# A decay tree's small products, issued in pairs of levels between the main products

## The reference: four blocks of mixer and feed-forward, the last two with two mixers

```python
def gla_chunked(q, k, v, g):      # q, k, g: (B, S, 4, 64); v: (B, S, 4, 128)
    ...
    b = jnp.cumsum(gc, axis=-2)
    diff = b[:, :, :, None, :] - b[:, :, None, :, :]
    decay = jnp.exp(jnp.where(causal[None, None, :, :, None], diff, -jnp.inf))
    attn = jnp.einsum('bhtk,bhsk,bhtsk->bhts', qc, kc, decay)
    o_intra = jnp.einsum('bhts,bhsv->bhtv', attn, vc)
    ...

def hybrid_mixer(h, w_in, ...):
    proj = h @ w_in               # queries, keys, values of both mixers, gates
    ...
    a_out = dilated_attention(aq, ak, av)
    o = gla_chunked(gq, gk, gv, log_alpha)
    return jnp.concatenate([a_out, g_out], axis=-1) @ w_out
```

## Time and profile before

| | |
|---|---|
| median of 3 runs | 1154.09 us (1153.79 to 1154.13) |
| span of the profiled execution | 1151.8 us |
| between span and median, outside the profile | 2.3 us |
| TensorE busy | 1140.5 us, 99% of the span |
| VectorE busy | 787.3 us, 68% |
| ScalarE busy | 602.4 us, 52% |
| levels of layer 2, of layer 3 | 584 to 627 us, 881 to 924 us |

### The profile page before, as it was taken

How to read it: one execution, slowest core, us unless ns; L and a number is a source line. 1 busy time by engine, 2 the same in 40 slices (tenths; PEclk the granted TensorE clock), 3 DMA queues, 4 the chain that set the end, 5 groups by cost and what they waited for, 6 DMA issues and landing times.

```text
span 1151.8 us, 18804 instructions
## 1 busy us (share of the span) xinstructions
PE 1140.5 (99%) x7018; PEld 932.6 (81%) x7018; DVE 787.3 (68%) x1166; ACT 602.4 (52%) x893; POOL 44.5 (4%) x71
## 2 busy tenths in 40 slices
PE   9999999999999999999999999999999999999998
PEld 7987888888868888888777788888887778888886
DVE  6798665558897865554789777556466977765641
ACT  5455544525964554442557665445356576554530
POOL 0120000000000000000100100000000010000000
PEclk9999999999999999999999999999999999999999
DMA  9756877645724687764576168777548524977650
GB/s 335 233 189 216 270 220 217 208 155 185 247 91 146 209 267 218 214 215 147 176 245 201 40 197 289 221 214 221 164 148 275 165 93 147 290 211 219 215 168 37
DMA packets 189066, 228.03 MB, mean 198 GB/s; under 512 B 16497, under 2 KB 132889, under 8 KB 188992
## 3 DMA queue, kind: packets, MB, share of 16 engines
q1 hardware_dynamic: 183600, 215.10, 59.2%
q10 hardware_dynamic: 5040, 11.64, 3.0%
q0 software_dynamic: 352, 0.30, 0.2%
HBM read 212.29 MB, written 1.06 MB: 185 GB/s over the span
## 4 chain that ended last, share of the span: by engine, by line
PE 48%; DVE 2%; ACT 0%; issue 0%; POOL 0%; POOLq 0%; DVEq 0%; ACTq 0%
PE ps L665 15%; PE ps L667 15%; PE ps L666 15%; DVE w_lo L1694 1%; PE ps L1055 1%; PE ps L1112 1%; PE ps L1137 0%; PE ps L859 0%; PE ps L1085 0%; PE ps L1104 0%; PE ps L1101 0%; DVE nbuf L2018 0%; PE ps L1084 0%; PE ps L878 0%; ACT w_hi L1291 0%
## 5 line engine op out<-in xcount | busy, mean ns | idle before, releaser
L1694 DVE TENSOR_TENSOR w_lo<-raw,w_hi 128x1024 fp32r<-128x1024 f32 x377 | 447.6, 1221 | 116.1 <-ACT w_hi L1291 112.7
L1291 ACT ACTIVATE w_hi<-raw 128x1024 fp32r<-128x1024 f32 x377 | 383.2, 1056 | 150.0 <-DMA raw<-w_down 34.0
L665 PE MATMUL ps<-w_hi,a_hi 128*128 128x512 f32 x991 | 390.3, 394 | 1.3 <-DVE a_lo L1717 0.7
L667 PE MATMUL ps<-w_hi,a_lo 128*128 128x512 f32 x991 | 386.0, 389 | 0.0
L666 PE MATMUL ps<-w_lo,a_hi 128*128 128x512 f32 x991 | 385.8, 389 | 0.0
L665 PEld LDWEIGHTS ps<-w_hi,a_hi 128*128 128x128 f32 x991 | 186.0, 188 | 42.9 <-DVE a_lo L1717 1.8
L667 PEld LDWEIGHTS ps<-w_hi,a_lo 128*128 128x128 f32 x991 | 186.0, 188 | 39.5
L666 PEld LDWEIGHTS ps<-w_lo,a_hi 128*128 128x128 f32 x991 | 186.1, 188 | 37.2
L665 PE MATMUL ps<-w_hi,h_hi 128*128 128x512 f32 x480 | 188.4, 392 | 0.5 <-DVE h_lo L2200 0.4
L667 PE MATMUL ps<-w_hi,h_lo 128*128 128x512 f32 x480 | 186.9, 389 | 0.0
L666 PE MATMUL ps<-w_lo,h_hi 128*128 128x512 f32 x480 | 186.8, 389 | 0.0
(11 more groups left out here) (229 smaller groups left out, 778.9 us busy)
## 6 DMA issues: line engine op xcount, KB each, us to landing
raw<-ffn_w_in SPq DMA_DIRECT2D x176, 256.0 KB, 3.9
raw<-w_in SPq DMA_DIRECT2D x96, 256.0 KB, 3.8
raw<-ffn_w_out SPq DMA_DIRECT2D x88, 256.0 KB, 3.1
raw<-w_gate SPq DMA_DIRECT2D x88, 256.0 KB, 3.4
raw<-w_up SPq DMA_DIRECT2D x88, 256.0 KB, 4.0
raw<-w_down SPq DMA_DIRECT2D x88, 256.0 KB, 3.3
moved<-turned SPq DMA_DIRECT2D x176, 64.0 KB, 2.6
raw<-od_w_in SPq DMA_DIRECT2D x40, 256.0 KB, 3.6
```

The source lines that it names most:

```text
L665: nc.tensor.matmul(ps[:, bank, :], hi, wh, start=first, stop=False)
L667: return nc.tensor.matmul(ps[:, bank, :], lo, wh, start=False, stop=last)
L1291: nc.scalar.activation(w_hi[:, v.slot, :], raw[:, v.slot, :], ACT.Copy).then_inc(w_high, 1)
L1694: V.tensor_tensor(w_lo[:, v.slot, :], raw[:, v.slot, :], w_hi[:, v.slot, :].bitcast(F32), ALU.subtract).then_inc(w_low, 1)
```

## The change: levels 1 and 2, 3 and 4, 5 and 6, 7 and 8 are issued together

Levels 2, 4, 6 and 8 write the upper half of the columns of the two banks, the others the lower half. So the second level of a pair needn't wait for the keep of the first, and TensorE issues both at one place. VectorE keeps the pair together, and a second keep waits until the first is done, since both write g_att. The work itself is the same: as many products, copies and subtractions as before.

```diff
-        LEVEL_STEP = ((2, 1), (2, 3), (3, 0), (3, 2), (3, 3), (4, 1), (4, 2), (5, 0), (5, 2))
+        LEVEL_STEP = {(2, 2): (0,), (3, 1): (1, 2), (4, 0): (3, 4), (4, 3): (5, 6), (5, 2): (7, 8)}
...
+        def level_half(n):
+            return 2 * P if n >= 2 and n % 2 == 0 else 0
...
-                        level(l, LEVEL_STEP.index((c, q)))
+                        for n in LEVEL_STEP[c, q]:
+                            level(l, n)
...
                     pe.wait_ge(g_scaled.sem, g_scaled.at(l, n - 1))
-                    pe.wait_ge(g_kept.sem, g_kept.at(l, n - 1))
+                    if n % 2:
+                        pe.wait_ge(g_kept.sem, g_kept.at(l, n - 1))
...
-                for n in LEVELS_AFTER.get(c, ()):
-                    level_distance(l, n)
-                    if n == 3:
-                        rope(l)
-                    keep(l, n)
-                    level_factors(l, n)
-                    feed(fed[0] + 1)
-                    if n in SQUARES_AFTER:
-                        for part, t in SQUARES_AFTER[n]:
-                            qk_squares(l, part, t)
+                if c == 1:
+                    level_distance(l, 0)
+                    level_factors(l, 0)
                     feed(fed[0] + 1)
+                    level_distance(l, 1)
+                    keep(l, 0)
+                    level_factors(l, 1)
+                if c == 2:
+                    level_distance(l, 2)
+                    rope(l)
+                    keep(l, 1)
+                    keep(l, 2)
+                    level_factors(l, 2)
+                    level_distance(l, 3)
+                    feed(fed[0] + 1)
+                    level_factors(l, 3)
+                    level_distance(l, 4)
+                    for t in range(NT):
+                        qk_squares(l, 0, t)
+                if c == 3:
+                    keep(l, 3)
+                    keep(l, 4)
+                    level_factors(l, 4)
+                    level_distance(l, 5)
+                    feed(fed[0] + 1)
+                    level_factors(l, 5)
+                    level_distance(l, 6)
+                    for t in range(NT):
+                        qk_squares(l, 1, t)
                 if c == 4:
+                    keep(l, 5)
+                    keep(l, 6)
+                    level_factors(l, 6)
+                    level_distance(l, 7)
+                    feed(fed[0] + 1)
+                    level_factors(l, 7)
                     feed(end - 2)
+                    keep(l, 7)
                     keep(l, NL)
                 feed(end)
...
-                dve.wait_ge(g_pair.sem, g_pair.at(l, n))
+                dve.wait_ge(g_pair.sem, g_pair.at(l, n + n % 2))
+                if n and n % 2 == 0:
+                    chain.settle()
+                    dve.wait_ge(g_kept.sem, g_kept.at(l, n - 1))
```

More of the change, by code:

```diff
@@ L536, in y_view @@
             return as_groups(ap) if LAYERS[l] == "hyb" else ap
-        LEVEL_STEP = ((2, 1), (2, 3), (3, 0), (3, 2), (3, 3), (4, 1), (4, 2), (5, 0), (5, 2))
-        SQUARES_AFTER = {4: ((0, 0), (0, 1)), 5: ((1, 0), (1, 1))}
+        LEVEL_STEP = {(2, 2): (0,), (3, 1): (1, 2), (4, 0): (3, 4), (4, 3): (5, 6), (5, 2): (7, 8)}
         QK_MOVES = {5: 0, 6: 1}
@@ L1030, in level @@
                     pe.wait_ge(g_scaled.sem, g_scaled.at(l, n - 1))
-                    pe.wait_ge(g_kept.sem, g_kept.at(l, n - 1))
+                    if n % 2:
+                        pe.wait_ge(g_kept.sem, g_kept.at(l, n - 1))
                 else:
                     pe.wait_ge(gqk_out.sem, gqk_out.at(l, 1))
+                left = level_half(n)
                 for b in range(2):
@@ L1051, in level @@
                                 ks = g_x[r, n % 2, b, here]
-                                qs, rows_k, col, w = right(ks, m), step, P // 2 * at + first // 2, step // 2
+                                qs, rows_k, col, w = right(ks, m), step, left + P // 2 * at + first // 2, step // 2
                                 if m >= 16:
@@ L2106, in keep @@
                         mask = right(const[:, C_LEVEL + P * (n - 2):C_LEVEL + P * (n - 1)].bitcast(I32), m)
-                        src = pair[:, 0:2 * P].rearrange("p (i j m) -> p i j m", i=4, m=m)
+                        left = level_half(n)
+                        src = pair[:, left:left + 2 * P].rearrange("p (i j m) -> p i j m", i=4, m=m)
                         ins = V.copy_predicated(dst, mask.unsqueeze(1).broadcast_to([P, 4, P // (2 * m), m]), src)
```

## The result

| | before, same chip | changed | ratio (95%) |
|---|---|---|---|
| median | 1153.94 us, 6 runs (1153.63 to 1154.56) | 1161.63 us (1158.89 to 1162.04) | 1.0059 (1.0048 to 1.0070) |
| the same kernel, a second series | 1154.39 us, 9 runs | 1160.56 us (1160.10 to 1161.47), 5 runs | 1.0055 (1.0042 to 1.0069) |

One further execution of the first series took 3205.5 us, has no trace, and is left out of the ratio; the 1161.63 still counts it, and without it the median is 1161.25. By the ratios, measured side by side, the change costs 0.55 to 0.59%, 6.3 to 6.8 us; by the medians, without the execution left out, 6.2 to 7.3. The forecast was 1157.5 with a range to 1159.6. The profiled execution is the shortest of its series, 1158.89 us with a span of 1157.1: 5.3 us above the span of before.

A forecast was written before the change was run, and what follows sets the result against it. TensorE and VectorE were taken as both full in the two stretches changed. VectorE's later maxima put the second logits 1.69 us later per layer, twice 3.4: span 1155.2, plus 2.3 around it 1157.5 us, range 1155.0 to 1159.6.

The forecast's parts named there:

- TensorE's lead at the end of the stretch: End of the 48-49 us the change touches in layers 2 and 3: keep 8 ends 628.47, first logits start 629.90.
- What TensorE saves: Four fewer departures from the main products per layer, 0.35 us each: 0 to 2.8 us over both layers, 2.8 taken.
- VectorE's walk: Step-by-step sum of VectorE's instructions through chunks 1 to 4 and into attention: second logits 1.69 us later; chance 0.62.
- The first wait for w_hi: Chunk 3: VectorE's subtraction right behind its distance (610.29) waits for ScalarE's high part until 612.02.
- the subtraction's loss beside GpSimd's copy: Chunk 3's three last subtractions: the queries' copy holds the shared port, delaying one of them by 0.83 us per layer.
- TensorE's wait inside the last pair: Before level 8: TensorE ready at 624.88, factors allow 626.89, so it waits 2.0 us in each layer.
- exp could start at 621.8, so it waits for VectorE instead: ScalarE's exp behind its copy of chunk 4 could start at 621.8, so VectorE's lateness there counts in full.
- The term of 1.73 us after the distance: Chunks 3 and 4: a subtraction needing the high part behind the exp can't start until 1.73 us after the distance.
- the 1.69 forecast: Loss per layer at attention's second logits: 633.98 instead of 632.29, 1.69 us later; twice that is 3.4 us.
- The hidden chain: Rival: level 8's factors ready by 624.9, so TensorE keeps its whole saving, 2.8 us off, 1151.3; chance 0.10.
- The port is missed: Rival: GpSimd's queries copy blocks no subtraction, 0.83 us less per layer, 1.7 in all, 1155.8; chance 0.13.
- More is late: Rival: a high part waits for its transfer or keeps run slower, one more microsecond per layer, 1159.5; chance 0.10.

The follow-up runs named there:

- experiment 4: Changed kernel with three unused 512-column float32 products put between levels 7 and 8, into TensorE's wait: 1159.35 us, ratio 1.0044.
- experiment 5: Changed kernel with VectorE reordered: in chunks 3 and 4 factors and distance precede the two keeps, last three subtractions go behind attention's maxima: 1151.81 us, ratio 0.9980.
- experiment 8: Changed kernel with high parts ahead of the exps of halvings 5 and 7, exp table loaded early, last two subtractions behind attention's maxima: 1151.84 us, ratio 0.9979.
- experiment 3: Changed kernel with the copy of the moved queries made by ScalarE, behind its copy of chunk 4, instead of GpSimd: 1158.56 us, ratio 1.0035.
- experiment 1: Changed kernel with an unused one-column exponential behind ScalarE's copy of chunk 4, so the exp table loads early: 1158.65 us, ratio 1.0036.
- experiment 10: Changed kernel with the exp table loaded early and two unused 512-column products in TensorE's wait before level 8: 1158.06 us, ratio 1.0034.
- experiment 9: Changed kernel run once more, unchanged, to profile an execution at a lower clock: 1160.56 us, ratio 1.0055.

## Why the prediction was wrong

**What bounds the kernel: right.** TensorE's lead at the end of the stretch was as short as read, and the loss came out there. From the second logits on, nothing was given back: 2.68 between the layers' second logits and 5.3 in the span are the same loss. The 2.3 us that the prediction put between span and median were two things: each execution's time is 1.8 to 1.9 us above its own span, and the profiled execution of before was some 0.5 us quicker than the median one (a span of 1152.3 belongs to the 1154.09, and 1151.8 to the profile). So the change's cost at full clock is nearer 5.1 us (1159.35 of experiment 4 less 1154.28) than 5.3.

**What TensorE saves: mis-sized, without effect.** 0.35 a detour was read as all of the level's time above its own products. Experiments 5 and 8 measure 0.28 to 0.30: 1.12 a layer by the trace, 2.4 us for eight by the medians. Some of the 0.35 stays between the levels of a pair: in experiment 5 levels 7 and 8 together begin 4.27 us ahead of the first logits (624.98 to 629.25), level 8 alone 3.62, and of the 0.65 more a level's own 64 products take 0.55. As the prediction said, it only lengthens or shortens the wait.

**VectorE's walk: right in its parts and 0.37 us short over 38 us.** The first wait for w_hi, the subtraction's loss beside GpSimd's copy (experiment 3: 0.84) and TensorE's wait inside the last pair are where they were put. 0.2 of the 0.37 was lost before the first wait ended; into which steps stays open.

**The step of the walk that failed is one sentence: "exp could start at 621.8, so it waits for VectorE instead".** I counted when ScalarE would be through with its copies, and took the table load as done by then. It stands behind the factors of halving 6, which the pairs move behind the copies. The term of 1.73 us after the distance measured 2.39 there, 0.66 more; experiment 1 moves the load and takes 0.70 off TensorE's wait, and experiment 10 0.69. So the layer's loss is the 1.69 forecast, 0.66 for the table and 0.37 of the walk: 2.72, against 2.68 measured. In the span: 1151.8 and twice 2.72 is 1157.2, against 1157.1. This alone would have left the time inside the forecast's range, near its upper end: 1159.35 in experiment 4.

**The step that took it out of the range was left out altogether: the clock.** The prediction put a wait of 2 us on TensorE twice and priced it at its length, at nothing more. Behind such a wait the granted clock fell in most executions. By the medians that cost 1.2 us in the second series (1160.56 less the 1159.35 of experiment 4) and 1.9 in the first (1161.25 less 1159.35); against the one execution at full clock, 1158.89, it would be 1.7 and 2.4. With the shorter wait of experiment 1 it is 0.6 (1158.65 less 1158.06 of experiment 10), which lies inside the spread of either series. The profiles, one execution each, give the same per layer, as us from the second logits of layer 2 to those of layer 3 (297.35 in the kernel before):

| kernel | clock holds | clock falls |
|---|---|---|
| changed | 300.03 (experiment 4: 300.01) | 300.51 (experiment 9) |
| with the table early | 299.35 (experiment 10) | 299.80 (experiment 1) |
| with ScalarE's copy of the queries | | 299.65 (experiment 3) |

So a fall in each layer costs about 0.5 us each time, since TensorE's slower work fills waits that it would have had anyway; the table costs 0.66 to 0.71, and GpSimd's copy 0.86. That products in the wait keep the clock at 0.999 and bring the spread from 3.2 and 1.4 down to 0.7 us is shown by experiments 4 and 10. What decides in which execution it falls is open: the profiled execution of the first series had the longer wait and kept its clock. Open too is what the executions of 1161 to 1162 us at 0.994 lost beyond the 0.996 of the one profiled with falls, 1160.10: none of them has a profile.

**The rivals.** The hidden chain did not come about in the changed kernel, but experiments 5 and 8 reach it by the order of VectorE or ScalarE, at 1151.8 where 1151.3 was worked out; most of the 0.5 is the saving's size (2.4 instead of 2.8). "The port is missed" fell: the copy came inside the three subtractions. "More is late" had nearly the size of the profiled execution (one more microsecond a layer, 1159.5) and other reasons than the true ones.

## What to carry to other kernels

When a change lets an engine wait where it had work, look at what its compiler-made instructions (here a table load of 1.28 us) stand behind: a cost hidden by the order of arrival comes out when the arrivals change places, and a dummy use of the table ahead of the wait hides it again. Where TensorE comes to wait some 2 us in one piece, as here, read the granted clock in small windows behind it in more than one execution, and price the wait with a range upward. Joining small products saved 0.28 us a detour here, but only once the engines that feed them were reordered with them: a pair needs both factors close together, and whatever stands between the two is in its way.

## What the runs showed of the hardware

- The clock fell to 0.50 around a wait of TensorE of 1.9 to 2.7 us, not at a fixed place: in experiment 1 at the end of the wait (0.92 in 626 to 628, the wait ending at 627.8), in experiment 9 about 1.5 us after TensorE was back at work. Main products went from 0.23 to 0.43 us apart, for about 3 us.
- The same program with the same waits of 2.7 us kept its clock in one execution (0.999) and had a lower mean in the nine others of usual length (0.994 to 0.996); the one of these with a profile shows the fall behind both waits.
- A fall behind each wait cost only about 0.5 us a layer in the end, though TensorE was 1.3 us later at the first logits: waits that it had behind the stretch were gone.
- A table load took 1.28 us, and the exponential started 1.30 us after the load did. Put ahead of the wait by an exponential of one column, the load no longer counted (experiment 1).
- A full-tile product of 16 columns between main products costs 0.21 us, a 64-row one 0.36; the main product behind either is recorded with 0.48 to 0.50 in place of 0.39, also where no tile size changes.
